# Moving x^T, the working region and the small tiles to other SBUF addresses in a four-layer fp32 kernel

## The reference, cut to what matters

```python
def even_layer(x, mem_n, ...):      # and odd_layer, with other mixing
    h = rmsnorm(x, ln_g)
    proj = h @ w_in                 # 2048 x 7192 (odd: 2048 x 7168)
    ...                             # neighbourhood attention, DeltaNet, memory attention
    return x + jnp.concatenate([na_o, dn_o, mem_o], axis=-1) @ w_out

def hybrid_layer(x, ...):           # twice
    h = rms_norm(x, norm_g)
    proj = h @ w_in                 # 2048 x 14416
    ...                             # MLA, SGU and GLA branches: y_a, y_b, y_c
    merged = (g[:, :, 0] * (y_a @ w_branch[0]) + g[:, :, 1] * (y_b @ w_branch[1])
              + g[:, :, 2] * (y_c @ w_branch[2]))
    return x + merged @ w_out
```

## Time and profile before

| | before |
|---|---|
| median of 3 runs | 3320.37 us (3318.04 to 3322.55) |
| the profiled execution, its own time | 3319.05 us |
| its span, first to last instruction | 3317.2 us |
| PE busy | 3200.5 us, 96% of the span |
| DVE, ACT busy | 1826.8 us (55%), 1523.0 us (46%) |
| mean granted TensorE clock | 0.973 of full speed |
| read from HBM | 523 MB, 161 GB/s over the span |

### The profile page before, as it was taken

One profiled execution on the slowest core, in us unless ns is written; L12 is line 12 of the kernel. 1 busy time (PEld: TensorE's weight loads), 2 busy tenths in 40 slices (PEclk: granted clock), 3 DMA queues, 4 the chain that ended last, 5 costly groups with the idle time before them and its releaser, 6 DMA issues.

```text
span 3317.2 us, 37434 instructions
## 1 busy us (share of the span) xinstructions
PE 3200.5 (96%) x15320; PEld 2653.7 (80%) x15320; DVE 1826.8 (55%) x2380; ACT 1523.0 (46%) x2334; POOL 10.4 (0%) x10
## 2 busy tenths in 40 slices
PE   7999999989988999999999999999999999999999
PEld 6877777778877788887887888888887887888887
DVE  4676655465654455474475545555474475545453
ACT  5544233354545554554445544444454445444442
POOL 0000000000000000000000000000000000000000
PEclk9899999999999999999899999999999899999999
DMA  7343222255644455553444555655553444555653
GB/s 258 119 150 122 72 64 89 83 166 165 222 144 142 128 200 179 189 185 109 145 163 150 193 194 193 214 183 185 181 190 103 153 164 142 189 191 190 216 189 141
DMA packets 274587, 535.28 MB, mean 161 GB/s; under 512 B 19024, under 2 KB 31440, under 8 KB 272112
## 3 DMA queue, kind: packets, MB, share of 16 engines
q1 hardware_dynamic: 270272, 509.12, 46.5%
q10 hardware_dynamic: 4144, 23.77, 1.8%
HBM read 523.41 MB, written 9.44 MB: 161 GB/s over the span
## 4 chain that ended last, share of the span: by engine, by line
PE 88%; DVE 5%; ACT 4%; DVEq 1%; issue 1%; DMA 0%; ACTq 0%; SPq 0%
PE acc L386 26%; PE acc L388 26%; PE acc L387 25%; PE tb L678 1%; DVE w_lo L349 1%; ACT w_hi L339 1%; PE tb L2197 1%; PE tb L868 1%; PE tb L875 1%; DVE c_out L779 1%; PE tb L2072 1%; PE tb L874 0%; PE tb L898 0%; PE tb L899 0%; PE tb L2070 0%
## 5 line engine op out<-in xcount | busy, mean ns | idle before, releaser
L349 DVE TENSOR_TENSOR w_lo<-raw,w_hi 128x1024 fp32r<-128x1024 f32 (+3 forms) x1016 | 1143.6, 1164 | 751.2 <-ACT w_hi L339 739.9
L339 ACT ACTIVATE w_hi<-raw 128x1024 fp32r<-128x1024 f32 (+3 forms) x1016 | 989.0, 1009 | 616.1 <-PE acc L388 599.3
L386 PE MATMUL acc<-w_hi,x_hi 128*128 128x512 f32 (+4 forms) x2912 | 1157.8, 398 | 15.3 <-DVE w_lo L349 15.3
L388 PE MATMUL acc<-w_hi,x_lo 128*128 128x512 f32 (+4 forms) x2912 | 1122.8, 386 | 0.0
L387 PE MATMUL acc<-w_lo,x_hi 128*128 128x512 f32 (+4 forms) x2912 | 1121.8, 385 | 0.0
L386 PEld LDWEIGHTS acc<-w_hi,x_hi 128*128 128x128 f32 x2912 | 568.8, 195 | 122.2 <-DVE w_lo L349 17.0
L388 PEld LDWEIGHTS acc<-w_hi,x_lo 128*128 128x128 f32 x2912 | 567.2, 195 | 108.2
L387 PEld LDWEIGHTS acc<-w_lo,x_hi 128*128 128x128 f32 x2912 | 568.8, 195 | 95.7
L386 PE MATMUL acc<-w_hi,mB_hi 128*128 128x512 f32 x256 | 101.8, 398 | 0.0
L387 PE MATMUL acc<-w_lo,mB_hi 128*128 128x512 f32 x256 | 101.0, 395 | 0.0
L388 PE MATMUL acc<-w_hi,mB_lo 128*128 128x512 f32 x256 | 101.0, 395 | 0.0
(11 more groups left out here) (482 smaller groups left out, 3574.0 us busy)
## 6 DMA issues: line engine op xcount, KB each, us to landing
raw<-in_h_w_in SPq DMA_DIRECT2D x224, 1024.0 KB, 5.0
raw<-in_o_w_in SPq DMA_DIRECT2D x56, 1024.0 KB, 5.2
raw<-in_e_w_in SPq DMA_DIRECT2D x48, 1024.0 KB, 5.0
raw<-in_h_w_branch SPq DMA_DIRECT2D x48, 1024.0 KB, 5.0
raw<-in_h_w_out SPq DMA_DIRECT2D x32, 1024.0 KB, 5.0
raw<-in_e_w_out SPq DMA_DIRECT2D x16, 1024.0 KB, 5.1
raw<-in_o_w_out SPq DMA_DIRECT2D x16, 1024.0 KB, 5.1
raw<-in_e_w_in SPq DMA_DIRECT2D x16, 512.0 KB, 3.6
```

Source lines behind the costliest of these rows:

```text
L339: act.activation(k.w_hi[:, a % HI_SLOTS, rows, :width], k.raw[:, a % SLOTS, rows, :width], ACT.Copy).then_inc(k.hi_ready, 1)
L349: e.tensor_tensor(k.w_lo[:, a % SLOTS, rows, :width], k.raw[:, a % SLOTS, rows, :width], k.w_hi[:, a % HI_SLOTS, rows, :width].bitcast(F32 ...
L386: pe.matmul(out, x_hi[:, tok], wh, start=first, stop=False)
L388: mm = pe.matmul(out, x_lo[:, tok], wh, start=False, stop=last)
```

## The change

The small tiles go first, at the beginning of the free SBUF. The three constant columns that were `one_eps` become the last of them, `const_cols`. The weight slots follow at the next multiple of 64 bytes, in the same inner order. Then 256 bytes are left unused, and `x_hi`, `x_lo` and the working region follow without a gap. The region has 64 words less, so the small tile `s_exp_` moves within it from word 23808 to word 23424. No instruction is added, removed or put elsewhere in the order; sizes and shapes are those of before.

Counting on again from 16512: `consts` at 23360 (320 modulo 512), weight slots at 35328 (0 modulo 512), `x_hi` at 101120 (256 modulo 512), working region at 133888 (256 modulo 512).

```diff
 def place_memory(k, nc, slab):
-    base = 0
     at = [slab]
...
-    k.raw = take("raw", [128, SLOTS, 4, CW], F32)
-    k.w_lo = take("w_lo", [128, SLOTS, 4, CW], F32R, slab)
-    k.w_hi = take("w_hi", [128, HI_SLOTS, 4, CW], F32R)
-    k.x_hi = take("x_hi", [128, KT, SEQ], F32R)
-    k.x_lo = take("x_lo", [128, KT, SEQ], F32R)
     small = at[0]
...
     k.pos_int = take("pos_int", [128, TILES], I32)
-    k.end = (at[0] + 31) // 32 * 32
-    at[0] = k.end
-    u = (at[0] + 32 + 63) // 64 * 64
-    k.u_base = u
+    k.const_cols = take("const_cols", [128, 3], F32)
+
+
+    slots = at[0] = (at[0] + 63) // 64 * 64
+    k.raw = take("raw", [128, SLOTS, 4, CW], F32)
+    k.w_lo = take("w_lo", [128, SLOTS, 4, CW], F32R, slots)
+    k.w_hi = take("w_hi", [128, HI_SLOTS, 4, CW], F32R)
+    at[0] += 256
+    k.x_hi = take("x_hi", [128, KT, SEQ], F32R)
+    k.x_lo = take("x_lo", [128, KT, SEQ], F32R)
+    u = at[0]
     k.u_words = (nc.sbuf_usable_end - u) // 4
...
-    k.s_exp_ = region("s_exp_", 23808, [128, 96])
+    k.s_exp_ = region("s_exp_", 23424, [128, 96])
...
-        place_memory(k, nc, (slab + 31) // 32 * 32)
-        one_eps = nc.alloc_sbuf_tensor_at("one_eps", [128, 3], F32, offset=k.end)
-        k.eps, k.one, k.eps_q = (one_eps[:, n:n + 1] for n in range(3))
+        place_memory(k, nc, (slab + 63) // 64 * 64)
+        k.eps, k.one, k.eps_q = (k.const_cols[:, n:n + 1] for n in range(3))
```

## The result

The changed kernel takes 3304.55 us (median of 5 runs, 3301.34 to 3307.40) against 3320.28 us (5 runs) before: 15.7 us less, ratio 0.9953 with a 95% interval from 0.9940 to 0.9966. The direction was the forecast's, the size was not: 77 us were expected, and 3304.55 us is the price given to the rival "256 acts like 0", 3303 us. The time does lie inside the stated range, which was wide enough to hold that rival.

What follows compares the result with a forecast made beforehand. TensorE, busy 96% of the span, was taken to bound the kernel by matmul count times pace. Savings of 44.9 us (x^T) and 36.6 us (region), together 81.5, times 0.95 made 77 us: 3243 us, range 3175 to 3350.

Steps and rivals of the forecast that it cites:

- 256 acts like 0: Rival for fills: period 256 bytes or a part; x^T stays at 226.7 ns, region gets there; 17 us, 3303 us, chance 0.16.
- the last part: Signs in the profile after: windows of fills alone show one pace for x^T and region tiles, about 221 ns.
- the region's term: Saving on the 3264 fills with region tiles, from 232.2 to 221 ns each: 36.6 us.
- The sum of 0: Whole change by the skill's rule: independent TensorE read ports, a load takes nothing from a running matmul, so no saving.
- I take half of what is on top of the floor for x^T: 221 ns: Pace of all 512-column fills at relation 256, estimated between 216 and 226.7 ns.
- x^T's 44.9 us: Saving on the 7872 fills with x^T as stationary operand, from 226.7 to 221 ns each.
- the 0.95: Share of each fill saving counted, because 5.4% of the time is at half clock, where nothing is on top.
- modulo 512 is the period: Operand placement in fills: 256 is half a period from x^T's 0, as far from the same place as possible.
- The reading of the floor as 216 ns: Lowest pace for 512-column fills, from plain fp32 matmuls of 256 columns; reaching it throughout gives 3190 us.
- The picture of two readers: TensorE's moving-operand and load reads hinder each other by placement, costing 13 ns (x^T) and 19 ns (region) per fill.
- 256 is worse than 0: Rival for fills: half a period apart is slower; 3361 us at the region's pace, 3444 at 240 ns; chance 0.30.

Runs made afterwards that it cites:

- region_only: Kernel before the change, in its own order, with only the working region's start moved 128 bytes later (`s_exp_` refitted): 3304.30 us, ratio 0.9958.
- d320: Changed kernel with x^T and region 320 bytes past the weight slots' rows in place of 256: 3364.42 us, ratio 1.0132 to before.
- d64: Changed kernel with x^T and region 64 bytes past the weight slots' rows in place of 256: 3364.08 us, ratio 1.0134 to before.
- d0: Changed kernel with nothing left unused ahead of x^T, so x^T and region at relation 0: 3305.78 us, ratio 0.9959 to before.
- x16: Changed kernel with x^T 16 bytes past the slots' rows modulo 256, region kept at 256: 3318.26 us, ratio 1.0000 to before.
- x240: Changed kernel with x^T 240 bytes past the slots' rows modulo 256, region kept at 256: 3306.39 us, ratio 0.9958 to before.
- d128: Changed kernel with x^T and region 128 bytes past the weight slots' rows in place of 256: 3353.03 us, ratio 1.0100 to before.

## Why the prediction was wrong

**Right:** the chain of reading. TensorE's pace bounds the kernel, and a change that issues nothing new moved the time through that pace alone. The count of 3264 region fills and 7872 x^T fills, the two paces 232.2 and 226.7, and the relation of the places (modulo 256, as it turned out) as the thing in which they differ, are borne out: region_only moves one address by 128 bytes and has all of the gain. After the change there is one pace for both kinds, as the last part asked. Splits, DMAs, `const_cols` and `s_exp_` cost nothing; the waits are those of before. The direction was right through the region's term alone. The Trainium skill (SBUF — State Buffer, "Who interferes with whom") gives TensorE independent read ports for the moving operand and for the load, and has it wait on no one. The sum of 0 that the prediction drew from this does not hold here: the same program at 64 and at 0 differs by 58 us. Whether it is the ports that fail to be independent, no run shows.

**Wrong:** the step "I take half of what is on top of the floor for x^T: 221 ns". The pace at 256 measured 226.7, exactly that at 0. Of the two terms, x^T's 44.9 us was nothing, and the region's 36.6 us was 5.5 x 3264 = 18.0, with the 0.95 17.1 us, where 15.7 was measured. The rest of 1.4 us is within the spread of the runs (3301.34 to 3307.40), and of the size of what 0.001 of mean clock makes: the profiled executions had 0.973 before and 0.972 after.

That step rested on two readings. The first was that modulo 512 is the period, so that 256 is as far from 0 as can be. It is not: d320 repeats d64 and d0 repeats the changed kernel, so 256 is 0. The hint was in the rows, and was used for the rival only: two known points, 0 and 384, don't tell 512 from 256, and a number that had been found by looking at the sizes of the rows was taken for one of the hardware. The second was that everything above 213.3 ns is two readers in each other's way, and can be placed away. The sweep finds nothing under 226.7 at ten relations, and less load does not bring less. The reading of the floor as 216 ns came from plain fp32 matmuls at half the columns per ns; nothing showed that fp32r at full pace can reach it, and nothing did.

The picture of two readers also had one of them twice as fast as the other, for which it showed no row; the earlier trace rows alone, 128 columns loaded in 0.19 us and 512 streamed in 0.227, would give more than three. The shorter loads bear the two out: a load takes 41.39 / 222 = 186 ns for 128 columns, 29.15 / 218 = 134 for 64 and 23.52 / 216 = 109 for 32, so each column more costs 0.8 ns, against 213.3 / 512 = 0.42 of the moving operand. Right as this was, what was built on it, that half a period apart is best, was not.

The slower rival, "256 is worse than 0", was wrong about 256, but its prices are those of the sweep: 3361 us for all at the region's pace, measured 3353 to 3365 us at 32, 64, 96 with 160, 128, 224 and 320.

**Open:** what the 13.3 ns at the best place are. Shorter loads do not take them away. They do not grow with the columns either. Fills of 384 columns, first in the changed kernel and then in d64, nine starts apart:

```profile
1385.28 0.33 PE L387 MATMUL acc<-w_hi,cT_hi 128*128 128x384 f32 x1
...
1386.84 0.33 PE L387 MATMUL acc<-w_hi,cT_hi 128*128 128x384 f32 x1
```

```profile
1405.08 0.34 PE L387 MATMUL acc<-w_hi,cT_hi 128*128 128x384 f32 x1
...
1406.64 0.34 PE L387 MATMUL acc<-w_hi,cT_hi 128*128 128x384 f32 x1
```

Both are 1.56 / 9 = 173.3 ns, where 384 columns at 2.4 GHz are 160: again 13.3 on top. So in the good place it looks like a fixed cost of each fill matmul. And the relation of 64, which costs 6.6 ns at 512 columns, costs nothing at 384. Open too is why two rhythms exist at one placement (x16, x240, d128), and what chooses between them; no rule is known that fits all the windows.

## What to carry to other kernels

For fp32r matmuls of 512 columns back to back, each with a load of 128 columns, the addresses of the stationary and the moving operand modulo 256 are worth up to 3% of the pace (226.7 against 233.3 ns): start both kinds of tile at the same place modulo 256, and check every group of fills by windows, since one layout can hold good and bad ones. At 384 columns a relation of 64 cost nothing, so the gain is not one of every shape. Two different paces of one instruction with one shape are a finding, and the cheap test is to move one tile, as the region's 128 bytes here. But the faster of two seen paces is the gain that is shown; the distance from it to a computed floor is not, until some row reaches the floor.

## What the runs showed of the hardware that was not expected

- The pace of a matmul of 512 columns depends on the relation of its operands' places modulo 256: 227 ns at 0 and 256, 227 to 228 at 240, 229 at 192, 232 to 233 at 128 and 384, 233 at 32, 64, 160, 224 and 320, 234 at 96.
- The absolute place has no part in what was tried: 128 with 128, 0 with 0 and 0 with 256 give one pace.
- At 16 bytes the same code ran at 227 ns in one layer and at 233 ns in another (222 and 216 matmuls in 50 us), each for the whole window.
- Fills of 384 columns start 173.3 ns apart at a relation of 256 and at 64 alike, 13.3 over 160 as the 512-column ones have 13.3 over 213.3 in the good place.
- Executions of one kernel differ with the granted clock: 3301.34 us at a mean of 0.973, 3307.40 at 0.971.
- A shorter load makes the matmuls no faster and in the good place slower: 230 ns with 64 columns and 231 to 232 with 32, against 226.7 with 128.
